# The 16-column gate projection moved out of the weight stream, into plain fp32 column groups

## The reference, cut to what matters

```
x = x + 0.5 * swiglu(rmsnorm(x, n1))
h = rmsnorm(x, n_mix)
qg, kg, vg, rg, a_low, qs, ks, vs = split(h @ w_in)      # widths 256 256 512 512 16 512 128 128
log_a = log_sigmoid(a_low @ w_a2 + b_a) / 16             # gate of the linear attention, 16 -> 256
o_g = gla_chunked(qg, kg, vg, log_a), normalised, * silu(rg)
o_s = sliding window attention with sinks (qs, ks, vs, partial rotary), rmsnorm
x = x + concat(o_g, o_s) @ w_out
x = x + 0.5 * swiglu(rmsnorm(x, n2))
```

## Time and profile before

| | |
|---|---|
| median of 3 runs | 1955.24 us (1953.77 to 1957.73) |
| profiled execution | 1954.67 us, its span 1952.8 us |
| TensorE busy | 1914.8 us, 98% |
| VectorE, ScalarE, GpSimd busy | 69%, 56%, 56% |
| granted TensorE clock, mean | 0.993 |

### The profile page before, as it was taken

One profiled execution on the slowest core, in us unless ns is written; L12 is line 12 of the kernel. 1 busy time (PEld: TensorE's weight loads), 2 busy tenths in 40 slices (PEclk: granted clock), 3 DMA queues, 4 the chain that ended last, 5 costly groups with the idle time before them and its releaser, 6 DMA issues.

```text
span 1952.8 us, 40743 instructions
## 1 busy us (share of the span) xinstructions
PE 1914.8 (98%) x15466; PEld 1886.5 (97%) x15466; DVE 1341.2 (69%) x2492; ACT 1098.3 (56%) x2230; POOL 1094.3 (56%) x811
## 2 busy tenths in 40 slices
PE   5999999999999999999999999999999999999997
PEld 5999999998999999999999999999999999999997
DVE  7975677576464986678678757865764568857774
ACT  4664566635344665466656646664453466646662
POOL 3666566732225666566766656666313266655663
PEclk9999999999999999999999999999999999999998
DMA  3233233331213232322323332333212222332331
GB/s 139 82 108 104 93 98 103 114 106 64 90 44 111 77 103 96 105 99 95 101 83 102 105 98 93 104 95 135 78 53 90 90 82 93 95 111 90 104 109 60
DMA packets 92114, 185.65 MB, mean 95 GB/s; under 512 B 12880, under 2 KB 22768, under 8 KB 91376
## 3 DMA queue, kind: packets, MB, share of 16 engines
q1 hardware_dynamic: 84096, 170.04, 26.5%
q10 hardware_dynamic: 7824, 13.00, 1.9%
HBM read 178.09 MB, written 6.95 MB: 95 GB/s over the span
## 4 chain that ended last, share of the span: by engine, by line
PE 93%; DVE 4%; ACT 1%; issue 1%; DMA 0%; POOLq 0%; POOL 0%; DVEq 0%; ACTq 0%
PE ps L819 57%; PE ps L779 23%; PE ps L828 7%; PE ps L1051 1%; PE ps L1040 1%; PE ps L807 1%; PE ps L1201 1%; PE ps L1023 1%; PE ps L799 0%; PE ps L1062 0%; DVE g_buf L2311 0%; PE ps L1164 0%; DVE h_end L1724 0%; DMA x<-xT 0%; DVE x L2375 0%
## 5 line engine op out<-in xcount | busy, mean ns | idle before, releaser
L819 PE MATMUL ps<-rhs,w_hi 128*128 128x272 f32 x4256 | 806.0, 289 | 0.0
L819 PEld LDWEIGHTS ps<-rhs,w_hi 128*128 128x128 f32 x4256 | 669.9, 188 | 1.4 <-DVE ssum L1911 1.1
L819 PE MATMUL ps<-rhs,w_lo 128*128 128x272 f32 x2128 | 613.8, 288 | 0.0
L656 POOL TENSOR_TENSOR w_lo<-w_raw,w_hi 128x512 fp32r<-128x512 f32 x272 | 351.0, 1295 | 253.0 <-ACT w_hi L1327 252.9
L819 PEld LDWEIGHTS ps<-rhs,w_lo 128*128 128x128 f32 x2128 | 402.3, 189 | 0.0
L650 POOL TENSOR_TENSOR w_lo<-w_raw,w_hi 128x1024 fp32r<-128x1024 f32 x80 | 191.4, 2394 | 353.3 <-ACT w_hi L1271 338.8
L819 PE MATMUL ps<-act_c,w_hi 128*128 128x272 f32 x1792 | 354.4, 289 | 1.1 <-DVE h_mid L1762 0.7
L656 POOL TENSOR_TENSOR w_lo<-s_tmp,w_hi 128x512 fp32r<-128x512 f32 x216 | 282.6, 1320 | 33.0 <-ACT w_hi L1327 32.8
L819 PEld LDWEIGHTS ps<-act_c,w_hi 128*128 128x128 f32 x1792 | 287.7, 188 | 1.8 <-DVE h_mid L1762 1.2
L779 PE MATMUL ps<-h_mid,w_hi 128*128 128x272 f32 x1600 | 279.3, 293 | 0.0
L819 PE MATMUL ps<-act_c,w_lo 128*128 128x272 f32 x896 | 258.2, 288 | 0.0
(11 more groups left out here) (292 smaller groups left out, 3182.7 us busy)
## 6 DMA issues: line engine op xcount, KB each, us to landing
w_raw<-stream SPq DMA_DIRECT2D x380, 256.0 KB, 2.9
w_raw<-stream SPq DMA_DIRECT2D x80, 512.0 KB, 3.3
g_buf<-stream SPq DMA_DIRECT2D x52, 256.0 KB, 2.8
pl_raw<-stream SPq DMA_DIRECT2D x64, 192.0 KB, 2.8
x<-xT ACTq DMA_DIRECT2D x8, 272.0 KB, 5.9
y_d<-x SPq DMA_DIRECT2D x8, 272.0 KB, 2.1
s<-s_d ACTq DMA_DIRECT2D x2, 1024.0 KB, 6.7
s_s_d<-s ACTq DMA_DIRECT2D x2, 1024.0 KB, 3.9
```

The source lines that it names most:

```text
L656: pool.tensor_tensor(operand(w_lo, j, half), source(op, s, half), operand(w_hi, j, half).bitcast(F32), ALU.subtract).then_inc(pool_low, 1)
L819: ins = pe.matmul(bank(s, at), w[:, k * P:(k + 1) * P], moving[:, k, side, r, :], start=fresh and k == 0 and w is hi and side == 0, stop=k ...
```

## The change

`a` no longer goes through the weight stream. Its weights (`w_in` columns 1536 to 1551, padded to 32) are loaded plainly into `w_in_a` (128 x 8 x 32, one DMA more in the "load" step), VectorE multiplies them by the norm's gain (`scale_a`, in slot 3), and TensorE multiplies them in plain fp32 by `x` itself. The output takes 32 partitions, so four blocks of the model width go to four column groups of the array: block `k0 + j` to partitions 32j to 32j+31. That is 16 matmuls of 128 x 32 by 272 columns. Each group holds a partial sum of two blocks; `z0` and `z1` now multiply all 128 rows of `aT` by four stacked copies of `wa`, which adds the groups up (the padding rows of the weights are zero). The two chunks of `a` leave the stream. `a` becomes job 7, `z0` job 9 directly ahead of `z1`, and `squares` moves one job back. The steps in the slots from 14 to 25 and the units from the fourth move one job index back as well. The chunk count per layer falls from 40 to 38, so ring slots are now computed with the layer (`ring_slot`), and the places of `s_tmp` go by layer instead of by half.

```diff
-IN_TILES = ["kS", "vS", "qS0", "qS1", "qS2", "qS3", "a", "kG0", "kG1", "qG0", "qG1",
+IN_TILES = ["kS", "vS", "qS0", "qS1", "qS2", "qS3", "kG0", "kG1", "qG0", "qG1",
...
-JOBS = ["kS", "vS", "qS0", "qS1", "qS2", "qS3", "a", "kG0", "z0", "kG1", "z1", "qG0", "qG1",
-        "vG0", "vG1", "vG2", "vG3", "rG0", "rG1", "squares", "rG2", "rG3"] + [f"out{n}" for n in range(KT)]
+JOBS = ["kS", "vS", "qS0", "qS1", "qS2", "qS3", "kG0", "a", "kG1", "z0", "z1", "qG0", "qG1",
+        "vG0", "vG1", "vG2", "vG3", "rG0", "rG1", "rG2", "squares", "rG3"] + [f"out{n}" for n in range(KT)]
...
+            3: [("rope", 2), ("scale_a", 0)],
...
-            18: [("att", 1), ("o", 0), ("kv", 2), ("kv", 3), ("o_norm", 0)],
-            19: [("s_norm", 0), ("smix", 0), ("smix", 1)],
-            20: [("att", 2), ("o", 1), ("kv", 4), ("kv", 5), ("o_norm", 1), ("smix", 2), ("smix", 3)],
+            19: [("att", 1), ("o", 0), ("kv", 2), ("kv", 3), ("o_norm", 0)],
+            20: [("s_norm", 0), ("smix", 0), ("smix", 1)],
+            21: [("att", 2), ("o", 1), ("kv", 4), ("kv", 5), ("o_norm", 1), ("smix", 2), ("smix", 3)],
...
-            25: [("gmix", 3), ("gmix", 4)],
+            26: [("gmix", 3), ("gmix", 4)],
             27: [("gs_kv", 0)],
...
-    unit_slots = [4, 5, 6, 7, 9, 11, 12, 13, 14, 15]
+    unit_slots = [4, 5, 6, 8, 11, 12, 13, 14, 15, 16]
...
-                                ins = pe.matmul(dst[:, hf, :], wa[0:16, pr * P:(pr + 1) * P],
-                                                aT[0:16, hf * TH:(hf + 1) * TH], start=True, stop=True)
+                                ins = pe.matmul(dst[:, hf, :], wa[:, pr * P:(pr + 1) * P],
+                                                aT[:, hf * TH:(hf + 1) * TH], start=True, stop=True)
...
+                        if name == "a":
+                            pe.wait_ge(m["wa_scaled"], 1)
+                            pe.wait_ge(part_kept, part_count(l, 0, KT - 1, 1))
+                            for k0 in range(0, KT, 4):
+                                for hf in range(2):
+                                    for j in range(4):
+                                        ins = pe.matmul(dst[j * 32:(j + 1) * 32, hf, :], w_in_a[:, k0 + j, :],
+                                                        x[:, k0 + j, hf * TH:(hf + 1) * TH], start=k0 == 0,
+                                                        stop=k0 > 0, skip_group_check=True)
+                            ins.then_inc(m["a_summed"], 1)
+                            continue
...
-                        act.dma_start(wa[0:16, :], wa2[l]).then_inc(m["loaded"], 16)
+                        act.dma_start(wa[:, :], wa2[l]).then_inc(m["loaded"], 16)
+                        act.dma_start(w_in_a[:, :, :], wa1[l]).then_inc(m["loaded"], 16)
...
+                        gain = lp[:, LG:LG + KT].unsqueeze(2).to_broadcast([P, KT, 32])
+                        dve.tensor_tensor(w_in_a[:, :, :], w_in_a[:, :, :], gain, ALU.mult).then_inc(m["wa_scaled"], 1)
```

More of the change, by code:

```diff
@@ L245, in trunk @@
         s_tmp = []
-        for half in range(2):
-            last = (2 * ((half * PL_H1 + PL_GU) % RING) + len(OPS)) % (2 * RING) * WB * 4
-            s_tmp.append([sb(f"s_tmp{half}{i}", [P, WB], at=plan["at"] - (2 - i) * RING * KT * P * 4 + last)
+        for l in range(DEPTH):
+            last = (2 * ring_slot(l, PL_GU) + len(OPS)) % (2 * RING) * WB * 4
+            s_tmp.append([sb(f"s_tmp{l}{i}", [P, WB], at=plan["at"] - (2 - i) * RING * KT * P * 4 + last)
                           for i in range(2)])
@@ L353, in source @@
             i = 0 if op == "S3" else 1
-            return s_tmp0[:, i, :] if s == 0 else s_tmp[half][i][:, :]
+            return s_tmp0[:, i, :] if s == 0 else s_tmp[l][i][:, :]
         def bank(s, i):
@@ L569, in block @@
                 done = blk_loaded[name + "ab"[s % 2] if name == "A22" else name]
-                sp.dma_start(source(name, s, half), stream[src, :, part:part + WB]).then_inc(done, 16)
+                sp.dma_start(source(name, s, l), stream[src, :, part:part + WB]).then_inc(done, 16)
             def after_sum(n, name):
@@ L879, in window @@
                         act_wait(l, half, s, "S2", NPAIR - 2)
-                        unit_product(half, s, op, range(NPAIR - 1))
+                        unit_product(l, half, s, op, range(NPAIR - 1))
                 for op in OPS:
@@ L900, in window @@
                         act_wait(l, half, s, op, NPAIR - 1)
-                        unit_product(half, s, op, range(NPAIR - 1, NPAIR)).then_inc(prod_done, 1)
+                        unit_product(l, half, s, op, range(NPAIR - 1, NPAIR)).then_inc(prod_done, 1)
                         continue
@@ L1530, in mixer @@
                                 high_part(l, c0 + CH_IN + n // 2 + RING)
-                        elif name[0] != "z" and name != "squares":
+                        elif name in IN_TILES:
                             if i == 0:
                                 root(l * 3 + 1)
-                            for part in range(2 if name == "a" else 1):
-                                c = in_chunk(name) + part
-                                high_part(l, c0 + c + RING)
+                            high_part(l, c0 + in_chunk(name) + RING)
                     elif step == "norm":
@@ L1771, in unit_sum @@
                     dve.wait_ge(staged, n * 2 + 1)
-                    first, second = ps[:, 6, 0:WB], source("A21", s, half)
+                    first, second = ps[:, 6, 0:WB], source("A21", s, l)
                 elif name == "S3":
@@ L1778, in unit_sum @@
                         dve.wait_ge(pool_low, n * 5 + POOL_LOW.index("S3") + 1 - 5)
-                    first, second = ps[:, 7, 0:WB], source("A21", s, half)
+                    first, second = ps[:, 7, 0:WB], source("A21", s, l)
                 elif name == "S2":
                     dve.wait_ge(sum_made, n * 4 + SUMS.index("S3") + 1)
-                    first, second = ps[:, 6, 0:WB], source("A11", s, half)
+                    first, second = ps[:, 6, 0:WB], source("A11", s, l)
                 else:
@@ L1785, in unit_sum @@
                     dve.wait_ge(sum_made, n * 4 + SUMS.index("S2") + 1)
-                    first, second = ps[:, 7, 0:WB], source("A12", s, half)
-                dve.tensor_tensor(source(name, s, half), first, second, ALU.add).then_inc(sum_made, 1)
+                    first, second = ps[:, 7, 0:WB], source("A12", s, l)
+                dve.tensor_tensor(source(name, s, l), first, second, ALU.add).then_inc(sum_made, 1)
             def unit_low(l, half, s, op):
@@ L2419, in tile @@
         return a.reshape(KT, P, -1).transpose(1, 0, 2)
[L2421 removed]
+    starts = {"qG": 0, "kG": 256, "vG": 512, "rG": 1024, "qS": 1552, "kS": 2064, "vS": 2192}
     for l in range(DEPTH):
@@ L2431, in weight_stream @@
             c = b + in_chunk(name)
[L2432 to L2436, removed]
             if name[:2] == "qS":
```

104 lines of the change are left out of this document (51 added, 53 removed).

## The result

The change made the kernel slower: median 1973.91 us (1972.21 to 1975.95, 5 runs) against 1955.24 us, a ratio of 1.0098 with a 95% interval of 1.0085 to 1.0111. That is 18.7 us more; forecast were 1969, 14 more, in a range of 1959 to 1977.

What follows compares the result with a forecast made beforehand. TensorE's program from start to end was taken as the bound (93% of the chain). Terms of -6.20 + 2.10 - 0.48 + 4.80 + 3.40 + 1.30 + 1.80 + 0.50 = +7.2 us a layer, +14.4 in both, gave 1969 us, range 1959 to 1977.

Steps and rivals of the forecast that it cites:

- I add nothing: Units, gate arithmetic and linear attention between slots 11 and 25: all one tile later, distances kept, so no added time.
- rival of two column groups at a time: New `a` matmuls: column groups do not all overlap, two at a time, +1.8 us a layer, 1973; chance 0.10.
- Column groups: New `a` block on TensorE: four groups at once, 1.82 us plus some 0.3 for start and division changes, 2.1 us.
- Gate products: `z0` and `z1` on TensorE: 1.74 us, like `squares`, instead of 2.22, so 0.48 us less a layer.
- First wait: TensorE ahead of `qG0`: stands still 4.80 us a layer, as VectorE does unit 3 before evacuating `z0`.
- Second wait: `out0` behind `smix`: TensorE waits 3.4 us a layer, 2.8 at the second quarter and then 0.6.
- the second pause of 0.6: Within `out0`: after the second quarter TensorE waits another 0.6 us, to 561.5, for `mix_ready`.
- Third wait: `gs_kv` behind `gmix`, which moved one output tile nearer: TensorE waits 1.3 us a layer.
- Clock: Falls to half clock: 1.8 us a layer at the wait ahead of `qG0`, 0.5 at `out0`.
- Small work: `scale_a` 0.36 us in VectorE's idle time, the new load 0.45 on ScalarE's queue, at most 0.1 us cost.

Runs made afterwards that it cites:

- the kernel with both moves (second run): Changed kernel with unit 3 moved behind z1 (slot 10) and `squares`, `smix` 2 and 3 back where they were, run again: 1948.10 us, 0.9977 of the kernel before.

## Why the prediction was right, and where a size was off

The three new waits, their causes, the overlap of the column groups and the two new falls of the clock were forecast and are there, and 1973.9 lies in the range. One step was wrong, the "I add nothing", and the clock was sized too small in one place. The number alone would not have told the forecast, 1969, from its rival of two column groups at a time, 1973, which is nearer; the 1.97 us of the block does. By the prediction's own steps, in us per layer (layer 0, layer 1 where they differ), matmul time from one start to the next:

| step | predicted | measured |
|---|---|---|
| tile `a` out, column groups in | -6.20 + 2.10 | -6.20 + 1.97 |
| gate products | -0.48 | -0.22 |
| wait ahead of `qG0` | +4.80 | +4.68 |
| clock in the `qG0` tile | +1.8 | +2.2, +1.3 |
| `out0`, wait and clock | +3.4 + 0.5 | +4.9 (8.00 for 3.11) |
| products behind `out0`, clock | 0 | +0.8, +0.2 |
| wait ahead of `gs_kv` | +1.3 | +1.3 |
| small waits | 0 | +1.6 |
| clock at `gs_o` | 0 | 0, -1.6 |
| sum | +7.2 | +11.0, +7.9 |

Measured from the first matmul of the norm's sums ahead of the mixer to that behind it, the two mixers are 246.06 - 235.38 = 10.7 and 241.43 - 233.79 = 7.6 us longer, 18.3 in all; the table is 0.3 to 0.4 above that, because one wait of the old order (0.4, transposes behind a score) is gone. Outside the mixers 0.4 us are left in all.

**Column groups.** Right: four at once. 32 instructions in 1.97 us are 62 ns each against 227 alone, 3.7 times as fast. The Trainium skill ("TensorE: Matmul & The Clock Gate", Part 3) gives 2.38 for three groups, and by the estimate made from it the block would have taken 2.6 us; here the share of the ideal is higher, 3.7 of 4.

The cost of changing the array's division is small. Behind the start of the block at most 1.97 - 8 x 0.227 = 0.15 us is left for it. Ahead of the block the 8 transposes take 436.00 - 434.97 = 1.03 us, where they took 435.21 - 434.36 = 0.85 ahead of a 128 x 128 tile in the kernel before:

```profile
434.36 1.09 PE L1040 MATMUL ps<-ident,sq_buf 128*128 128x128 f32 x8
435.21 0.50 PE L779 MATMUL ps<-h_mid,w_hi 128*128 128x272 f32 x2
```

Together that is 0.33 us, latency included, beside the 0.3 of the prediction. The drain that the Trainium skill names ("TensorEngine Tiling (Array Packing)", Key Properties) costs no more than that here. The 0.18 ahead of the block is not in the table; about as much falls away ahead of the gate products, which now fill all 128 rows.

**Gate products.** Mis-sized by 0.26: `z0` and `z1` together take 2.00 us, not the 1.74 that `squares` gave. With the wait behind them it is 454.36 - 447.68 = 6.68 us for 6.54.

**First wait.** Right to 0.1 us, since VectorE's chain was taken over whole; moving the unit took it away, with 13.7 us.

**Second wait.** The wait was right (2.60 measured for the 2.8 of the second quarter), but the second pause of 0.6 did not come: at half clock the quarter itself took 570.57 - 569.04 = 1.53 us, which covers it. The clock was mis-sized. I gave it 0.5 us; `out0` took 8.00 us where wait and matmuls at full clock give 6.5, so 1.5, and 0.8 and 0.2 more in the products behind it.

**Third wait.** Right, 1.29 for 1.3. Moving `gs_kv` one tile later gained nothing, since another wait took its place.

**"I add nothing" for the steps between slot 11 and slot 25.** This step failed, by 1.6 us a layer. Its premise, that all of them come one tile later, does not hold, and "the steps in the slots from 14 to 25 move one job index back" in the description of the change is too broad as well: `vtr` 0 to 2, `keys`, `decay` 1 and `gate` 1 stay in slots 13 to 15, while the units, `samp_s`, `samp_t` and all that follows move. `vtr` 0 now comes behind the short `pv` of unit 4 and asks for vG0 before it is evacuated (0.4). `samp_t` lost `vtr` 2 as its cover (0.6). Moving the transposes showed both. The wait for `oT` (0.6) is read from the trace only: `o` 3 now stands behind `out1`, and ScalarE makes a chunk's high part for odd outputs alone, so 1.04 us of that stand ahead of its squares; no experiment took it away.

**Clock.** Its parts sum to 2.2 + 1.5 + 0.8 = 4.5 us in layer 0 and 1.3 + 1.5 + 0.2 - 1.6 = 1.4 in layer 1; predicted were 2.3 in each. That the total came within 5 us is in part luck: the 1.6 us that the shorter fall behind `gs_o` gave back in layer 1 was in no term, and it made up for half of the 3.2 us of small waits, which were in none either. That the two large waits bring falls was right in both layers. How long a fall lasts differs between the layers of one execution, and no run shows what decides it; that stays open.

**Small work.** `scale_a` took 0.42 us on VectorE, the added load 0.45 on ScalarE's queue; no wait names either.

The best version found keeps the new `a` and moves unit 3, `squares` with `smix` 2 and 3, and `vtr` 0 to 2: 1943.73 us, 0.9956 of the kernel before. Of the 2 x 4.45 us of matmul time saved it still pays 1.3 at `gs_kv` and 0.6 at `oT` in each layer.

## What to carry to other kernels

When a long step in a program of a fixed order becomes short, ask first whose latency it covered. Take the chain of the other engines whole from the trace (from TensorE's own starting instruction to the end of the evacuation that it will wait for) and subtract what is left on TensorE in between; here that gave 4.80 for 4.68. Moving a step by one place in such a list moves its cover as well, so each pair of neighbours has to be looked at, the small ones too; in this kernel three such moves were worth 30 us, some of it the clock's, and the cheaper product 9.

## What the runs showed of the hardware

- Four column groups of 32, each with all 128 rows and its own data of 272 fp32 columns, run side by side: the first four instructions start within 20 ns, 32 take 1.97 us, and one after another they would take 32 x 0.227 = 7.3. That was so with the groups issued in turn. One group after another took 4.79 us: the second group's first instruction started only together with the first group's fifth, ahead of three of the first group that stand before it in the program.
- In the changed kernel the granted clock fell to half at both large pauses of TensorE, 4.68 and 2.60 us, in both layers, and cost 1.3 to 2.2 us in the `qG0` tile. But the 3.46 us pause of the new `a` in the old order brought a fall in layer 1 alone (mean clock 0.66 from 1386 to 1396 us); in layer 0 the clock stayed full (1.00 from 431 to 441 us).
- The clock also falls at the little matmuls of `gs_o`, with no pause at all (in the kernel before TensorE was busy all the time from 528.1 to 532.4 us, at a mean clock of 0.50), and what that costs differs between kernels and between layers of one execution. The tile behind took 8.3 and 7.2 us in the two layers of the changed kernel; in layer 1 it took 7.5 us in the kernel with both moves (second run) and 6.6 with the transposes moved as well.
